# A two-block transformer kernel on one core: the taps of the causal convolution are summed by accumulating transfers instead of GpSimd additions

## The reference, cut to what matters

```python
def conv_module(u, cv_w, cv_b, ln_w, ln_b):
    a, b = jnp.split(u, 2, axis=-1)
    h = a * jax.nn.sigmoid(b)
    h = lax.conv_general_dilated(h, cv_w[:, None, :], window_strides=(1,),
        padding=[(CV_WIDTH_FILTER - 1, 0)], dimension_numbers=('NWC', 'WIO', 'NWC'),
        feature_group_count=CV_WIDTH) + cv_b
    mu, var = mean and variance over the channels
    return silu((h - mu) * rsqrt(var + EPS) * ln_w + ln_b)
```

## Time and profile before

| | |
|---|---|
| median of 3 runs | 1393.64 us |
| profiled execution | 1392.23 us, span 1390.0 us |
| TensorE, VectorE, ScalarE, GpSimd busy | 92%, 63%, 42%, 14% of the span |
| mean granted TensorE clock | 0.967 |
| traffic | 137.87 MB, mean 99 GB/s |

### The profile page before, as it was taken

One profiled execution on the slowest core, in us unless ns is written; L12 is line 12 of the kernel. 1 busy time (PEld: TensorE's weight loads), 2 busy tenths in 40 slices (PEclk: granted clock), 3 DMA queues, 4 the chain that ended last, 5 costly groups with the idle time before them and its releaser, 6 DMA issues.

```text
span 1390.0 us, 18986 instructions
## 1 busy us (share of the span) xinstructions
PE 1279.1 (92%) x6581; PEld 1025.8 (74%) x6581; DVE 870.9 (63%) x1249; ACT 590.1 (42%) x834; POOL 201.5 (14%) x200
## 2 busy tenths in 40 slices
PE   6899478999899999999999998999999989989697
PEld 2678356778688788788888876888788867767476
DVE  4779988766765422344444886674466567767763
ACT  3475543551443211343333555442233336577542
POOL 6038864000000000000000000110011002233100
PEclk9999789999899999999999999999999999999899
DMA  8553212423545333233332222333222313223131
GB/s 304 152 178 87 61 47 62 122 76 121 153 138 151 105 98 98 82 100 92 100 96 76 76 82 84 89 93 103 79 81 86 106 54 100 81 68 91 34 102 61
DMA packets 204436, 137.87 MB, mean 99 GB/s; under 512 B 7074, under 2 KB 191569, under 8 KB 204384
## 3 DMA queue, kind: packets, MB, share of 16 engines
q1 hardware_dynamic: 200784, 134.40, 32.5%
q0 software_dynamic: 1376, 1.73, 0.4%
q10 hardware_dynamic: 2224, 1.05, 0.3%
HBM read 135.06 MB, written 2.10 MB: 99 GB/s over the span
## 4 chain that ended last, share of the span: by engine, by line
PE 62%; DVE 21%; ACT 7%; issue 7%; DMA 2%; DVEq 0%; ACTq 0%; SPq 0%
PE banks L386 19%; PE banks L387 19%; PE banks L388 19%; DVE w_lo L370 3%; ACT w_hi L358 2%; DVE xc L2168 1%; PE banks L1032 1%; DVE t_s L2188 1%; DMA raw<-in_ada_w 1%; DVE score L1731 1%; DVE score L1714 1%; DVE m L1728 1%; DVE vt L2079 1%; DVE e L2077 1%; ACT e L1487 1%
## 5 line engine op out<-in xcount | busy, mean ns | idle before, releaser
L370 DVE TENSOR_TENSOR w_lo<-raw,w_hi 128x1024 fp32r<-128x1024 f32 x204 | 264.1, 1302 | 175.2 <-ACT w_hi L358 172.6
L386 PE MATMUL banks<-h_hi,w_hi 128*128 128x512 f32 x824 | 332.6, 404 | 15.1 <-issue 4.7
L387 PE MATMUL banks<-h_lo,w_hi 128*128 128x512 f32 x824 | 324.6, 394 | 0.0
L388 PE MATMUL banks<-h_hi,w_lo 128*128 128x512 f32 x824 | 324.4, 394 | 0.0
L358 ACT ACTIVATE w_hi<-raw 128x1024 fp32r<-128x1024 f32 x204 | 213.0, 1052 | 166.2 <-PE banks L388 145.2
L386 PEld LDWEIGHTS banks<-h_hi,w_hi 128*128 128x128 f32 x824 | 157.4, 191 | 56.4 <-issue 13.4
L387 PEld LDWEIGHTS banks<-h_lo,w_hi 128*128 128x128 f32 x824 | 157.4, 191 | 33.9 <-issue 2.4
L388 PEld LDWEIGHTS banks<-h_hi,w_lo 128*128 128x128 f32 x824 | 157.0, 191 | 33.6
L386 PE MATMUL banks<-n_hi,w_hi 128*128 128x512 f32 x256 | 103.1, 403 | 1.2 <-DVE xT L1936 1.2
L386 PE MATMUL banks<-hid_hi,w_hi 128*128 128x512 f32 x256 | 102.7, 401 | 0.0
L387 PE MATMUL banks<-hid_lo,w_hi 128*128 128x512 f32 x256 | 102.4, 400 | 0.0
(11 more groups left out here) (374 smaller groups left out, 1983.1 us busy)
## 6 DMA issues: line engine op xcount, KB each, us to landing
raw<-in_mlp_w SPq DMA_DIRECT2D x64, 512.0 KB, 4.0
raw<-in_a_w_in SPq DMA_DIRECT2D x48, 512.0 KB, 3.9
raw<-in_ada_w SPq DMA_DIRECT2D x40, 512.0 KB, 4.3
raw<-in_w_in SPq DMA_DIRECT2D x28, 512.0 KB, 3.8
raw<-in_b_w_in SPq DMA_DIRECT2D x24, 512.0 KB, 3.9
raw<-in_a_w_out SPq DMA_DIRECT2D x16, 512.0 KB, 3.7
raw<-in_b_w_out SPq DMA_DIRECT2D x16, 384.0 KB, 3.3
raw<-in_w_out SPq DMA_DIRECT2D x8, 512.0 KB, 4.4
```

The costliest lines, as they stand in the source:

```text
L370: dve.tensor_tensor(dst, src, hi, ALU.subtract).then_inc(split_lo, 1)
L386: pe.matmul(dst, l_hi, r_hi, start=first, stop=False)
L387: pe.matmul(dst, l_hi, r_lo, start=False, stop=False)
L388: return pe.matmul(dst, l_lo, r_hi, start=False, stop=last)
```

## The change

The additions leave GpSimd's arithmetic and become transfers from SBUF to SBUF that add to their destination, issued from GpSimd's queue (`dma_start(..., accum_op=ALU.add)`). There are two sums: the even ones go on in `cacc`, the odd ones in `codd`, two tiles of `omix` that are free until the mixers' outputs are written. Tap 0 with the bias starts the even sum and tap 1, written by ScalarE, the odd one, so 29 taps for each m are left to the transfers: 15 into the even sum, 14 into the odd one. A transfer waits for the landing of the one before it on the same sum. Behind the last of an m GpSimd waits for both sums and adds the odd to the even by one more transfer; `tapped` now counts those two. Each transfer moves 128 rows of 2 KB (256 KB). The slots, the four buffers and the rule of reuse stay: ScalarE waits until the product four places earlier has landed.

```diff
+        codd = omix[:, 6:8, :]
+        PER_M = TAPS - 2
+        EVEN_PER_M, ODD_PER_M = (PER_M + 1) // 2, PER_M // 2
+
+        def sum_of(n):
+
+            m, j = divmod(n, PER_M)
+            if j % 2:
+                return odd_summed, codd, m * ODD_PER_M + j // 2
+            return even_summed, cacc, m * EVEN_PER_M + j // 2
...
             def conv_mean():
-                pe.wait_ge(tapped, N_PRODUCTS)
+                pe.wait_ge(tapped, 16 * CVT)
...
                     h = (c - C_HG) // P
-                    act.wait_ge(tapped, N_PRODUCTS)
+                    act.wait_ge(tapped, 16 * CVT)
...
                     act.activation(cacc[:, m, :], hpad[:, m, 0:TOK], ACT.Identity, bias=pcol("cv_b", m), scale=pcol("cv_w", m))\
                        .then_inc(first_tap, 1)
+                    act.activation(codd[:, m, :], hpad[:, m, 1:1 + TOK], ACT.Copy, scale=pcol("cv_w", CVT + m))\
+                       .then_inc(first_tap, 1)
+                    return
+                n = m * PER_M + k - 2
                 if n >= 4:
-                    act.wait_ge(tapped, n - 3)
+                    summed, _, o = sum_of(n - 4)
+                    act.wait_ge(summed, 16 * (o + 1))
...
             def add_product(n):
 
-                m = n // (TAPS - 1)
-                pool.wait_ge(first_tap, m + 1)
+                m, k = divmod(n, TAPS - 1)
+                if k == 0:
+                    return
+                n = m * PER_M + k - 1
+                summed, into, o = sum_of(n)
+                pool.wait_ge(first_tap, 2 * m + 2)
                 pool.wait_ge(weighted, n + 1)
-                if n:
-                    pool.wait_ge(tapped, n)
-                pool.tensor_tensor(cacc[:, m, :], cacc[:, m, :], weighted_tap(n), ALU.add).then_inc(tapped, 1)
+                if o:
+                    pool.wait_ge(summed, 16 * o)
+                pool.dma_start(into[:, m, :], weighted_tap(n), accum_op=ALU.add).then_inc(summed, 16)
+                if k == TAPS - 2:
+                    pool.wait_ge(even_summed, 16 * EVEN_PER_M * (m + 1))
+                    pool.wait_ge(odd_summed, 16 * ODD_PER_M * (m + 1))
+                    if m:
+                        pool.wait_ge(tapped, 16 * m)
+                    pool.dma_start(cacc[:, m, :], codd[:, m, :], accum_op=ALU.add).then_inc(tapped, 16)
```

More of the change, by code:

```diff
@@ L304, in build @@
         conv_gated, first_tap, weighted, tapped = sem("conv_gated"), sem("first_tap"), sem("weighted"), sem("tapped")
+        even_summed, odd_summed = sem("even_summed"), sem("odd_summed")
         mean_made, cen_made, csq_made, var_made = sem("mean_made"), sem("cen_made"), sem("csq_made"), sem("var_made")
```

## The result

The changed kernel takes 1404.08 us (median of 7 runs, 1400.9 to 1408.02) against 1393.74 us of the kernel before in the same number of runs: ratio 1.007, 95% interval 1.0051 to 1.0089. The forecast was 1379 us and faster. The time lies inside the stated range, on the side of rival 2.

A forecast was written before the change was run, and what follows sets the result against it. VectorE, hindered by GpSimd's additions, was taken to bound the convolution stage. Of a 29 us ceiling, serial landings left 14.4: 1392.23 less 14.4 is 1377.8, plus 1.4 for the median, so 1379 us; range 1366 to 1409.

The forecast's parts named there:

- rival 2: Slots 15 to 20: landings become the bound and TensorE starves; slower, 1404 us at L = 5.0; chance 0.29.
- What bounds the kernel before: Convolution stage: VectorE holds the end, its operations lengthened by GpSimd's additions; removing them gains at most 29 us.
- the ceiling: Most that VectorE's relief could gain: 21 us before the levels and 8 in them, 29 us together.
- The relief of VectorE: 84 to 230 us: without GpSimd's additions VectorE's operations return to quiet lengths, 37 us less, not all on the path.
- Rival 3: Transfers keep up but VectorE is not relieved, as GpSimd's issuing takes the same port; 1389 to 1398 us; chance 0.05.
- The form of the added cost: Each sum is a chain of serial landings; slot 21's split starts at 122.1 + 21 L.
- The step: Products 12 to 52: 21 serial landings of 3.8 us, each with 0.17 us to the next issue.
- The start: Slot 9: GpSimd stands at the third mask at 113.5 us instead of 122.0, earlier products landed or nearly so.
- L: Landing time of one 256 KB adding transfer, taken as 3.8 us; ceiling reached at 3.1, no gain at 4.48.

The follow-up runs named there:

- experiment 1: The kernel before the change, each of its 60 GpSimd additions cut to one column, so the convolution's sum is left out: 1363.4 us, ratio 0.9777.
- experiment 4: The changed kernel with one sum instead of two, every transfer waiting for the one before: 1494.6 us in one run.
- experiment 5: The changed kernel with each of the 58 adding transfers cut to 128 of 512 columns (64 KB): 1379.8 us, ratio 0.9892.
- experiment 8: The changed kernel with three sums, one by transfers and two by GpSimd's additions, and the first m's join moved later: 1394.5 us, ratio 0.9997.

## Why the prediction was wrong, point by point

**What bounds the kernel before** was right: taking the additions away (experiment 1) gives 32 us on one chip (1395.7 to 1363.4), where the ceiling was put at 29, and slot 21's split comes at 188.7 where the sum had 187.3.

**The relief of VectorE** was right in kind and size: decays at 479 ns where 423 was taken, one 384 wide form of L1714 at 619 for 616 (the other, beside GpSimd's remaining arithmetic, at 1002), the remainder at a median of 1226; 32.8 us less busy where 37 was counted. Rival 3 is refuted by these rows. TensorE's wait for the last decay fell from 17.8 to 9.5 us, not to a few.

**The form of the added cost** was right: the split of slot 21 hangs on serial landings, and the chain of waits shows them one behind another. ScalarE's weighted taps waited 63.8 us for landings in 84 to 232 us, where they had waited 26.6 for additions (the 16.4 of the earlier trace rows are those into `sqb` alone). **Its size was the error.** The prediction had 201.9 us for that split; it came at 229.93, 28.0 late. The terms:

- *The step.* From product 12 to product 52 the sum had 21 landings of 3.8 ("I take 3.8"), 21 times 0.17 and two of GpSimd's three gate products (the first stands ahead of product 12), 86.0 us. From the issue of product 12 (125.14) to ScalarE's tap that waited for product 52 (229.30) are 104.2 us, 18.2 more. The chain of waits has 20 landings in it, 89.2 us together and 4.46 in the mean (4.3 is the median of all), where 79.8 stood: 9.4 of the 18.2. Between them lie 15.0 us where 6.2 stood: the other 8.8. Of these 15.0, 9.5 are 17 times 0.56 us from a landing to the next issue, for which 0.17 was taken; 5.5 lie where GpSimd's order held the next issue, at the first step, the seam and 192.70. The gate products, counted as 2.6, lie behind landings and cost nothing there. Smaller terms at both ends take 0.3 off, which makes 17.9 us.
- *The start.* "By then the 12 products of slots 5 to 8 have landed or nearly so", and the third mask at 113.5. It stands at 123.62 us, 10.1 later: 3.0 of that came from ahead of slot 6, 7.1 is pacing that I had not let begin so early. The chain of waits is on landings from 95.43 us; ScalarE waited 4.55 us in slot 7 and 2.79 in slot 8 for them.

17.9 + 7.1 + 3.0 = 28.0. The two failing terms alone turn a gain of 14.4 into a loss of 10.6; the profiles show 10.7 in the stretch. The landing by itself would not have turned the sign: with 4.46 for L the prediction's own sum gives 215.8 us, level with 216.25. So rival 2 had the right place and the right sign, but its condition, L from 4.6 on, was not met; the time to the next issue and the early start made the loss.

Why was 3.8 wrong, when rival 2 with its decision point was on the page? The value was the landing of copies of the same total bytes in a stretch of 0.19 to 0.35 load. But the transfers were to raise that load themselves: at 1.6 us of all engines for each and one product in 2.5 us, they are busy for 0.64 of the time by themselves, which with the 0.19 to 0.27 of before makes about the 0.85 to 0.88 measured, and the weights (`in_w_in`) went from 3.8 to 4.8 us in turn. Alone on its chain such a transfer lands in 3.3 us (experiment 4), less than I took; two chains make it 4.3, and with a quarter of the bytes it is 3.3 again (experiment 5). And the 0.17 us was read from one GpSimd operation to the next; from the landing of a transfer to the next issue GpSimd needs 0.56. Whether that would be shorter with another form of wait was not tried.

## What to carry to other kernels

An accumulation by transfers is a chain, and its price is the number of serial landings times the landing and the time to the next issue, taken under the load that the transfers themselves make: work out their engine time and add it to the load before taking a duration from a quiet stretch. Where GpSimd's arithmetic hinders VectorE on the path, neither all of it on GpSimd nor all of it in transfers was best here, but two chains of transfers and one of GpSimd side by side, 0.9908 of the time (three chains of transfers with the joins on GpSimd have 0.9937, and the two intervals touch). A mean over few operations can hide a single long one: look at the median and the longest beside it. And a wait "for the one before" by a count that two tiles share also orders the tiles.

## What the runs showed of the hardware that was not expected

- GpSimd's issue of an adding transfer takes 0.86 us, of a copy 0.54 (the issue of `gw` took 0.53).
- An adding transfer of 256 KB occupies the 16 engines for 1.6 us, a copy of the same size for 0.71 and an adding one of 64 KB for 0.59: a quarter of the bytes takes more than a third of the time.
- A 256 KB copy between two places in SBUF over GpSimd's queue lands in 2.2 us at best and 3.4 in the median beside the weights. The Trainium skill's sum for such a transfer, 2.0 us and its bytes at 436 GB/s ("DMA: Bandwidth & Descriptors", Anatomy of one DMA, SWDGE path), makes an estimate of 2.6 us; here that lies between the best and the median, and below every adding one of that size, 3.2 at the least.
- One VectorE operation of 1.23 us took 11.85 us beside 16 us of GpSimd work without a pause (experiment 8).
